# A hybrid decoder step on eight cores: Tanh as the gate, another turn of the first loads, the squares of 28 norms summed on GpSimd, and the mixer's bias on VectorE

## The reference, cut to what matters

```python
for i in range(2):                                   # layer 0: RG-LRU, layer 1: chunked gMLP
    h = h + mixer_i(rmsnorm(h, norm_mix[i]))
    h = h + conv_ffn(rmsnorm(h, norm_ffn[i]))        # up 1024->6144, causal conv of 3, gelu(g)*u, down
    gate = sigmoid(rmsnorm(h, norm_ple[i]) @ ple_w_gate[i])
    h = h + gate * (p[i] @ ple_w_proj[i])            # the "PLE" stage
out = rmsnorm(h, norm_final)

rmsnorm(x, g) = x * rsqrt(mean(x * x, axis=-1) + 1e-6) * g
lru_mixer: proj = xn @ w_in; gate, xb = split(proj); xc = causal_dwconv(xb)     # 4 taps
           r, i = sigmoid(xc @ w_a + b_a), sigmoid(xc @ w_x + b_x)              # 4 heads of 256
           h_t = a_t h_{t-1} + sqrt(1 - a_t^2) (i_t x_t);  y = (gelu(gate) * h) @ w_out
gmlp_mixer: u, v = split(gelu(xn @ w_in)); v = layernorm(v)
           s[t] = sum_s tril(w_s[g])[t, s] v[s] + b_s[g, t]                     # 128-token chunks
           y = (u * s) @ w_out
```

## Time and profile before

| | |
|---|---|
| median of 3 runs | 1787.09 us |
| profiled execution | 1787.4 us, of which 1785.8 in the span |
| spans of the 8 cores | 1776.7 to 1785.8 us, granted clock 0.981 to 0.984 |
| PE busy | 1691.7 us, 95% of the span, 11096 matmuls |
| DVE, ACT, POOL busy | 1223.3 (69%), 1015.9 (57%), 446.6 us (25%) |
| the chain that ended last | PE 79%, ACT 7%, issue 5%, DVE 5%, DMA 2%, POOL 1% |
| ACT table loads | 156, 200.1 us |

### The profile page before, as it was taken

One profiled execution on the slowest core, in us unless ns is written; L12 is line 12 of the kernel. 1 busy time (PEld: TensorE's weight loads), 2 busy tenths in 40 slices (PEclk: granted clock), 3 DMA queues, 4 the chain that ended last, 5 costly groups with the idle time before them and its releaser, 6 DMA issues.

```text
span 1785.8 us, 35476 instructions; the slowest of 8 cores (1776.7 to 1785.8 us)
## 1 busy us (share of the span) xinstructions
PE 1691.7 (95%) x11096; PEld 1076.0 (60%) x11096; DVE 1223.3 (69%) x2544; ACT 1015.9 (57%) x1995; POOL 446.6 (25%) x897
## 2 busy tenths in 40 slices
PE   4799999799999999999899999999999999999985
PEld 2466656466666666666555556666666666666654
DVE  2566656997767676776657666787676776677666
ACT  3877779654444444479944432854434444449984
POOL 1533333311111111112354222201111111112343
PEclk8899999999999999999999999999999999999997
DMA  8800030045031221200272000403140404030023
GB/s 173 172 27 1 1 64 14 1 85 103 13 59 28 46 46 27 48 13 1 58 137 53 1 1 1 85 3 60 37 72 1 72 1 72 1 60 1 1 75 130
DMA packets 21675, 82.44 MB, mean 46 GB/s; under 512 B 1778, under 2 KB 12850, under 8 KB 15604
## 3 DMA queue, kind: packets, MB, share of 16 engines
...
## 4 chain that ended last, share of the span: by engine, by line
PE 79%; ACT 7%; issue 5%; DVE 5%; DMA 2%; POOL 1%; DVEq 0%; ACTq 0%; POOLq 0%; SPq 0%
PE PS L582 79%; ACT SB L530 4%; DVE SB L566 3%; ACT L530 2%; DVE SB L541 1%; DMA SB<-xT 1%; POOL SB L541 1%; DMA SB<-lru_w_x_in 1%; ACT PS L530 1%; ACT SB L571 1%; POOL SB L557 0%; DVE SB L557 0%; DVE SB L1296 0%; DVE SB L970 0%; DVEq L293 0%
## 5 line engine op out<-in xcount | busy, mean ns | idle before, releaser
L582 PE MATMUL PS<-SB 128*128 128x352 bf16 (+6 forms) x11096 | 1691.7, 314 | 87.3 <-ACT SB L530 40.9
L582 PEld LDWEIGHTS PS<-SB 128*128 128x128 bf16 x11096 | 1076.0, 98 | 702.8 <-issue 131.1
L541 DVE TENSOR_TENSOR SB<-SB,PS 128x352 bf16<-128x352 f32 (+6 forms) x1112 | 532.1, 512 | 164.9 <-PE PS L582 106.0
L566 DVE SCALAR_TENSOR_TENSOR SB<-SB 128x352 f32<-128x352 f32 (+1 forms) x720 | 380.8, 548 | 218.1 <-ACT SB L571 200.2
L530 ACT ACTIVATE SB<-PS,SB 128x352 f32<-128x352 f32 (+1 forms) x432 | 257.0, 616 | 366.4 <-PE PS L582 353.2
L530 ACT ACTIVATE SB<-SB 128x352 f32<-128x352 f32 (+6 forms) x678 | 314.7, 501 | 174.5 <-DVE SB L566 134.0
L573 POOL COPY SB<-SB 128x2 f32<-128x2 f32 (+2 forms) x472 | 150.7, 323 | 778.8 <-ACT SB L571 651.6
L541 POOL TENSOR_TENSOR SB<-SB 128x352 f32<-128x352 f32 (+6 forms) x242 | 230.2, 965 | 269.0 <-DVE SB L541 153.0
L566 DVE SCALAR_TENSOR_TENSOR SB<-SB,PS 128x352 bf16<-128x352 f32 (+6 forms) x344 | 174.2, 565 | 111.4 <-ACT PS L530 110.3
L530 ACT ACT_TABLE_LOAD x156 | 200.1, 1283 | 60.7 <-PE PS L582 48.5
L530 ACT ACTIVATE SB<-PS 128x352 f32<-128x352 f32 (+8 forms) x234 | 107.2, 472 | 125.9 <-PE PS L582 99.4
...
## 6 DMA issues: line engine op xcount, KB each, us to landing
...
SB<-ple_w_gate POOLq DMA_DIRECT2D x2, 2048.0 KB, 14.6
...
SB<-lru_w_x_in POOLq DMA_DIRECT2D x4, 512.0 KB, 12.5
```

The lines of the kernel that those rows point to most:

```text
L541: emit(eng, lambda e: e.tensor_tensor(out=out.ap, in0=a.ap, in1=b.ap, op=op), R=[a, b], W=[out], cost=c)
L566: emit("dve", lambda e: e.scalar_tensor_tensor(out=out.ap, in0=a.ap, scalar=sa, in1=b.ap, op0=op0, op1=op1), R=rr, W=[out], cost=c)
L582: emit("pe", lambda e: e.matmul(ps.ap, lhsT=lhsT.ap, rhs=rhs.ap, start=start, stop=stop), R=[lhsT, rhs], W=[ps], cost=max(0.05, 0.000427 * ...
```

## The change

It has five parts.

1. In 28 norms (nf0 of tiles 2 to 5, all of np0, nm1, nf1 and np1) the squares are written in f32 into four scratch tiles (two for nf1 of tile 0), GpSimd adds them up in 7 additions, the last of which writes bf16, and a single matmul against `onesD` follows. The 6 norms of the LRU mixer, nf0 of tiles 0 and 1, and the 7 final ones stay as they were.
2. The gMLP bias is loaded as 128 equal rows (`bsB`, 512 KB) and added on DVE, PSUM to SBUF; the bias matmuls and the preparation of `bsR` are gone. The product with u goes to GpSimd for groups 0, 2 and 4, and stays on DVE for 1, 3, 5, 6 and 7. Groups of u and spatial groups take turns, with a lead of 3 groups (7 in tile 0).
3. The PLE gate is computed as 0.5 (1 + tanh(x/2)): Tanh on ACT, (t + 1) times the projection on DVE, and the projection weights are halved once for each layer.
4. The first loads come in another turn, and the squares of the LRU norms of tiles 1 and 2 are made on DVE.
5. `t16`, a scratch of the LRU mixer for the sample columns, gets eight tiles in a region of its own; it was one, in the region that later holds the normed tile 3.

```diff
@@ norm
+            if isinstance(sqs, tuple):
+                off, nf = sqs
+                ps = banks(n)
+                fv = [T(mem, [n], F32, off=off + i * n * 4).all() for i in range(nf)]
+                at = [0] + [1 + (c - 1) % (nf - 1) for c in range(1, KC)]
+                total = T(mem, [n], BF16, off=off + (1 + (KC - 1) % (nf - 1)) % nf * n * 4).all()
+                for c in range(KC):
+                    act(fv[at[c]], hv(c, c0, n), AF.Square)
+                    if 0 < c < KC - 1:
+                        tt(fv[0], fv[0], fv[at[c]], ALU.add, eng="pool")
+                    if c % 2 == 1:
+                        yield
+                tt(total, fv[0], fv[at[KC - 1]], ALU.add, eng="pool")
+                yield
+                mm(ps, onesD.all(), total, True, True)
...
         for q in range(4):
-            load("pool", lw_x.v(q), kp(w_lx_in[q], KC), K("lwx%d" % q), hblock(2, 4, 0, TN) if q == 0 else None)
-        load("pool", lw_a.all(), kp(w_la, KC), K("lwa"))
+            load("pool", lw_x.v(q), kp(w_lx_in[q], KC), K("lwx%d" % q), hblock(2, 4, 0, TN) if q == 1 else None)
+        load_x(1, 2, lw_x.v(1))
+        load("pool", lw_a.all(), kp(w_la, KC), K("lwa"), hblock(0, 8, TN, TN))
         load("pool", lw_i.all(), kp(w_lx, KC), K("lwi"))
-        load_x(1, 2, lw_x.v(1))
         for q in range(2):
-            load("pool", lw_g.v(q), kp(w_lg_in[q], KC), K("lwg%d" % q), hblock(0, 8, TN, TN) if q == 0 else None)
-        load_x(2, 2, lw_i.all())
+            load("pool", lw_g.v(q), kp(w_lg_in[q], KC), K("lwg%d" % q))
+        load_x(2, 2, lw_g.v(0))
         load("pool", lw_o.all(), kp(w_lout, KC), K("lwo"), hblock(0, 8, 2 * TN, TN))
-        load_x(3, 2, lw_g.v(1))
+        load_x(3, 2, lw_o.all())
...
@@ pproj weights, once for each layer
+                for k in range(2):
+                    ts(slot.pproj.v(k), slot.pproj.v(k), 0.5, ALU.mult)
...
@@ xn_norm
-            if sqs is not None:
-                sqs = [s.v((0, n)) for s in sqs]
+            if sqs is None and presum:
+                sqs = (XN[ti].off, 4)
...
-        bg.append(("lru", lru_norm(1, "act")))
-        bg.append(("lru", lru_norm(2, "pool")))
+        bg.append(("lru", lru_norm(1, "dve")))
+        bg.append(("lru", lru_norm(2, "dve")))
...
-        t16 = r5([NSEQ], F32)
+        t16 = rl([8, NSEQ], F32)
...
@@ the PLE step
-            act(th, ps, AF.Sigmoid)
-            tt(th, th, pp, ALU.mult)
+            act(th, ps, AF.Tanh, scale=0.5)
+            stt(th, th, 1.0, pp, ALU.add, ALU.mult)
             tt(hv(m, c0, n), hv(m, c0, n), th, ALU.add, eng="dve" if ti in short else "pool")
...
@@ g_S
-            for g in range(8):
+            def u_group(g):
                 psu = B7(n)
...
+            lead = 7 if ti == 0 else 3
+            for g in range(lead):
+                u_group(g)
             for g in range(8):
...
-                mm(V(pss.ap[:, 0:npr].rearrange("p (q t) -> p q t", t=128), pss.bufs), on,
-                   V(bb.ap.unsqueeze(1).broadcast_to([33, nq, 128]), bb.bufs), True, False)
...
+                tt(s3, p3, V(bb.ap.unsqueeze(1).broadcast_to([128, nq, 128]), bb.bufs), ALU.add)
...
-                tt(ggate.v(g, (0, n)), uv, pss, ALU.mult)
+                tt(ggate.v(g, (0, n)), uv, sv, ALU.mult, eng="dve" if g % 2 or g == 6 else "pool")
+                if ti > 0 and g + lead < 8:
+                    u_group(g + lead)
```

More of the change, by code:

```diff
@@ L669, in build_program @@
         assert ra.o <= TOFF + 32768
-        PREG = T(mem, [2, NTOK], BF16, off=SB_BYTES - 5120 - 2 * NTOK * 2)
+        PREG = T(mem, [2, NTOK], BF16, off=SB_BYTES - 7168 - 2 * NTOK * 2)
         assert ra.o <= PREG.off, (ra.o, PREG.off)
-        TAIL = Region(SB_BYTES - 5120, 5120)
+        TAIL = Region(SB_BYTES - 7168, 7168)
         wsTm = TAIL([KC, 128], BF16)
         bd = TAIL([KC, 64], BF16, parts=64)
-        bsR = TAIL([1024], BF16)
+        bsB = TAIL([KC, 128], F32)
         rp = Region(TOFF + 32768, PREG.off - TOFF - 32768)
-        th2 = rp([TN], F32)
         ggate = rp([KC, 384], BF16)
-        ubuf = [rp([384], F32) for _ in range(3)] + [T(mem, [384], F32, off=PREG.off + i * 1536) for i in range(5)]
+        th2 = T(mem, [TN], F32, off=ggate.off)
+        ubuf = [rp([384], F32) for _ in range(3)] + [T(mem, [384], F32, off=PREG.off + i * 1536) for i in range(4)]
         gw_v = T(mem, [KC, D], BF16, off=TOFF)
@@ L690, in build_program @@
         vT = [rx([D], BF16) for _ in range(4)]
-        gsq = [rx([TN], BF16) for _ in range(4)]
+        gsq = rx([2, TN], F32)
+        sbuf = [rx([384], F32), T(mem, [384], F32, off=PREG.off + 6144)]
         yout = [T(mem, [KC * TN], F32, off=TOFF + i * KC * TN * 4) for i in range(2)]
-        bsf = T(mem, [D], F32, off=ggate.off, parts=64)
-        maskb = T(mem, [128], BF16, off=ggate.off + 4096)
-        m64b = T(mem, [64], BF16, off=ggate.off + 4352, parts=64)
+        maskb = T(mem, [128], BF16, off=ggate.off)
+        m64b = T(mem, [64], BF16, off=ggate.off + 256, parts=64)
         lw_x = T(mem, [4, KC, 256], BF16, off=S_OFF[0])
@@ L757, in norm @@
         def norm(c0, n, gname, outs, sqs=None, sqeng="act", after=None, banks=BN, order=None, done=None):
+            if isinstance(sqs, tuple):
[13 more added lines that the diff above has]
+                mm(ps, onesD.all(), total, True, True)
+                yield
+                act(ps, ps, AF.Ln, bias=epsT.all(), order=[] if order is None else order())
+                last = act(ps, ps, AF.Exp, scale=-0.5)
+                if done is not None:
+                    done(last)
+                yield
+                for c in range(KC):
+                    stt(outs[c], hv(c, c0, n), vcol(gname, c), ps, ALU.mult, ALU.mult)
+                    if c % 2 == 1:
+                        yield
+                if after is not None:
+                    after()
+                return
             if sqs is None:
@@ L825, in build_program @@
         mset(epsT.all(), EPS)
-        mset(ones1.all(), 1.0)
         mset(phalf.all(), -0.5)
@@ L965, in chain_step @@
                 b3 = V(s4(thi[c].v((npr, n))).ap[:, :, 0], thi[c].v((npr, n)).bufs)
-                tt(t16.all(), a3, h0s.v(c), ALU.mult)
-                tt(b3, b3, t16.all(), ALU.add)
+                tt(t16.v(c), a3, h0s.v(c), ALU.mult)
+                tt(b3, b3, t16.v(c), ALU.add)
                 mset(a3, 0.0)
@@ L1002, in build_program @@
                 gen = lru_norm(ti + 1, ["act", "pool"] * 4) if ti + 1 < 6 else xn_norm(
-                    "nf0", 0, None, ["act", "pool"] * 4, order=lambda: phase("exp"), done=lambda op: keep("rstd", op))
+                    "nf0", 0, None, ["act", "pool"] * 4, False, order=lambda: phase("exp"), done=lambda op: keep("rstd", op))
                 bg.append((nb, gen))
@@ L1038, in build_program @@
                 exp_step(ti, c)
-        bg.append(("xn", xn_norm("nf0", 1, None, ["act", "pool"] * 4, order=lambda: phase("exp"), done=lambda op: keep("rstd", op))))
+        bg.append(("xn", xn_norm("nf0", 1, None, ["act", "pool"] * 4, False, order=lambda: phase("exp"), done=lambda op: keep("rstd", op))))
         for c in range(KC):
@@ L1248, in g_prep1 @@
         def g_prep1():
-            load("sp", bsf.v(p=(0, 1)), bsrow, K("bsf"))
-            load("sp", bsf.v(p=(32, 33)), bsrow, K("bsf2"))
+            load("sp", bsB.all(), bsrow.rearrange("p (g t) -> p g t", g=8), K("bsf"))
             load("pool", wsTm.all(), wsT_d.rearrange("p (g t) -> p g t", g=8), K("wsT"))
@@ L1269, in g_norm @@
             n = npr + ns
-            return norm(c0, n, "nm1", [gxn[ti % 2].v(c, (0, n)) for c in range(KC)])
+            return norm(c0, n, "nm1", [gxn[ti % 2].v(c, (0, n)) for c in range(KC)], (gxn[ti % 2].off, 4))
         vcnt = [0]
@@ L1373, in build_program @@
             else:
-                bg.append(("xn0", xn_norm("nf1", 0, gsq)))
+                bg.append(("xn0", xn_norm("nf1", 0, (gsq.off, 2))))
                 g_S(ti)
```

33 lines of the change are left out of this document (16 added, 17 removed).

## The result

The changed kernel takes 0.9924 of the time before, with a 95% interval of 0.9901 to 0.9948: 1787.3 x 0.9924 = 1773.7 us, 13.6 us (0.8%) less. Its undisturbed runs took 1773.26 and 1774.49 us; in two others the clock of a die was lower, and they are left out of the ratio. The prediction was 1735, its range 1716 to 1760. The direction was right, the size a quarter of it. The profiled execution took 1774.49 us with a span of 1772.9.

The account below looks back on a forecast made before the run. TensorE's matmuls were taken to bound the kernel (busy 1691.7 of 1785.8 us). Terms -29.3 - 7.2 - 8 - 10 - 4 + 6 = -52.5 took 1787.4, less 0.3, to 1735 us, range 1716 to 1760.

Parts of the forecast that it names:

- Matmuls removed, -29.3 and -7.2: On TensorE: 7 matmuls fewer in each of 28 norms save 29.3 us, the gMLP's 56 bias matmuls 7.2 us.
- most of the 2.6 us more is covered: A GpSimd sum takes 6.6 us against about 4; other groups cover most, so 3 us were charged for all sums.
- the sign of late sums: TensorE's waits on GpSimd's L541 beyond 5 us would show that the sums come late.
- The tail, +2: At the kernel's end about 4 us more of DVE's work stand late, behind 15 final products: 2 us lost.
- Bias, -7.2 + 1: In the gMLP: 56 bias matmuls gone save 7.2 us by width (far end 17); 1 us of cost there.
- Tables, -8: In the PLE stretches: Tanh shares Gelu's set, 51 table loads go from ACT, TensorE gains 8 us (3 to 16).
- The start, -10: First 90 us: earlier first loads and squares off ACT cut TensorE's standstill by 10 us (0 to 22).
- The rival that the loads' new turn gives it back: At the start: a chain of transfers replaces the standstill, so nothing is gained, 1749 us; chance 0.18.
- some 6 to 8 can be kept: At tile 0's gates: of two waits' 13.4 us, 6 to 8 are saved although `lru_w_a` is issued later.
- The LRU's end, -4: End of the LRU mixer: with `t16` elsewhere a wait for DVE's memset goes, about half gained, 4 us (0 to 8).
- that of the late sums: At TensorE: GpSimd's sums come 1 us late in each of 28 norms, 1760 us; chance 0.12.
- The lock: Each GpSimd addition of a norm waits for one DVE product, sums 4.1 us later, up to 1847 us; chance 0.04.

Follow-up runs that it names:

- r12: The kernel before with the gMLP part alone (bias on DVE, products shared with GpSimd, u and spatial groups in turn): 1777.3 us.
- r2: The changed kernel with the gMLP mixer's spatial part as before, the norms' sums on GpSimd kept: 1776.6 us.
- r3: The changed kernel with all 28 norms back to 8 matmuls each, without GpSimd's 196 additions: 1761.4 us.
- r5: The kernel before with the sums on GpSimd in the same 28 norms and nothing else: 1791.1 us.
- r8: r3 plus 7 GpSimd additions for each of 24 norms (np0, nm1, nf1, np1), whose results nobody reads: 1776.6 us.
- r7: The changed kernel with the final norms of tiles 3, 4 and 5 in other PSUM banks, the last PLE steps having five banks: 1761.6 us.
- r4: The kernel before with the Tanh gate alone in place of Sigmoid, projection weights halved: 1780.0 us.
- r1: The changed kernel with the start as before (order of first loads, squares of LRU norms 1 and 2 on ACT and GpSimd): 1773.4 us.
- r14: r10 with the whole start as before (loads in the old turn, squares of LRU norms 1 and 2 on ACT and GpSimd): 1752.5 us.
- r10: The changed kernel with the sums in np0 alone (6 norms) and the final norms' other PSUM banks: 1752.6 us.

## Why the prediction was wrong

- **Matmuls removed, -29.3 and -7.2**: the counts were right (10,844 matmuls, 196 and 56 fewer), and the 34.4 us of busy time gone for 36.5 are near by luck. The bias matmuls freed 16.2 us alone (1691.7 to 1675.5 in r12) and 14.5 beside the sums (r2), twice the 7.2; those of the sums freed 17.1 (r3 to the changed kernel) and 12.3 alone (1691.7 to 1679.4 in r5), where 29.3 was written. A part of it is the clock: TensorE stood more, and the granted clock fell from 0.983 to 0.977, and from 0.981 to 0.975.
- **The step that failed** is the next one: "most of the 2.6 us more is covered", +3 for all 28 sums. r3 against the changed kernel has it at +30.2 us of standstill, and 12.2 us of busy time that did not go. Together they put the sums, matmuls included, at +12 us, not -26: 38 of the 39 us by which the forecast missed. By the marks of these two traces they lose 5.1 us at the end of the LRU mixer, 7.4 in the mixer, 9.5 in the tail, gain 6.7 in the first PLE stretch, and 1 each in A and E.
- **The rest of the sum** came out near, in part by luck: without the sums and their cost it was -28.2, 1759 us, and r3 took 1761.4. But the start gave 0 for -10, and the bias more than was written.
- **Why it failed**: I priced only the delay of a sum at TensorE. The waits on GpSimd are 6.6 us, as small as I said, and no larger than without the sums (8.2 in r3). That they would pass 5 us was to be the sign of late sums, and it tells nothing. But beside the additions DVE was busy 35.4 us longer (1230.6 to 1266.0), its SBUF products slower (0.581 to 0.909 us), and where it had little room (17 of 20 us at the mixer's end) TensorE waited for DVE. The row that told of it, 0.754, stood in the prediction. That these rows' contention is the whole of it isn't shown: the tail's part is the bank, the part at the LRU's end is open, and of the mixer's r8 has only some 4 us from load alone.
- **A busy TensorE is not a covered one**: in the mixer 40 matmuls fewer left its busy time at 192.3 us (192.4 in r3), at a granted clock (of 2.4 GHz; the lower level is 1.2) of 0.97 for 0.99, so the matmuls removed there gained nothing.
- **The tail, +2**: it cost 9.6, through the bank (r7 took 15 away). A place that was named, and mis-sized since I looked for DVE's backlog and not at what the next final norm waits for.
- **Bias, -7.2 + 1**: -10.0 alone (r12), -3 beside the sums (r2). Both terms were mis-sized, the gain by my choice of the row (15.8) and the cost (5.8 us of standstill alone for 1).
- **Tables, -8**: -7.3 (r4). Tanh shares Gelu's set: 104 loads, where about 105 were counted. By the list in the Trainium skill, "ScalarE: Activation LUTs", section "Table sets: the hidden batching unit", taken for this Gelu, nothing would have been gained; the page itself keeps the approximated Gelu apart, and the runs show it in one set with Tanh.
- **The start, -10**: 0 (r1; r14 against r10). The rival that the loads' new turn gives it back was right; it had 0.18. The "some 6 to 8 can be kept" rested on an issue of `lru_w_a` at 28 us, and it came at 34.87. Its sign came too: 31.4 us of standstill in the first 90.
- **The LRU's end, -4**: about -3, B being 99.5 us before and 96.2 without sums; no run undid `t16` by itself. With the sums TensorE waited 7.03 us there again, for DVE; in r3 its longest wait for DVE's L541 is 3.5 us, so that wait came with the sums and not, as "what is late next" said, with DVE's own chain.
- **The rivals**: that of the late sums was the nearest (1760, 0.12), but by another mechanism, and it bounded the cost at 28 us where 38 were lost. The lock's mechanism was there in kind, at a smaller price: it charged each addition with a wait of 0.58 us, and the rows have an addition at 1.03 us for 0.94 and a product 0.33 us longer.
